# Seven steps of small products in a gated recurrence, gathered into three, with four more gathers on GpSimd

## The reference

```python
def chunked_gated_recurrence(q, k, log_f, v):
    """S_t = diag(f_t) S_{t-1} + k_t v_t^T,  o_t = S_t^T q_t  (chunkwise form)."""
    ...

def hgrn2_mixer(h, w_in, w_out, g_norm_w, lb_fwd, lb_bwd):
    """Bidirectional HGRN2. Single combined input projection partitioned into
    [q | f_fwd | f_bwd | i | g]; one scan per direction, summed; gated RMSNorm; output projection."""
    ...
    o = rmsnorm(o, g_norm_w) * jax.nn.silu(gh.astype(jnp.float32))
    return o.reshape(B_, L, D).astype(h.dtype) @ w_out
```

## Time and profile before

| | us |
|---|---|
| median of 3 runs | 2721.85 (2720.99 to 2722.36) |
| the profiled execution | 2721.11 |
| its span, first to last instruction | 2718.9 |
| TensorE busy | 2700.7 (99%) |
| DVE busy | 1966.1 (72%) |
| ACT busy | 1331.5 (49%) |
| GpSimd busy | 89.6 (3%) |
| DMA, mean over the span | 177 GB/s |

### The profile page before, as it was taken

One profiled execution on the slowest core, in us unless ns is written; L12 is line 12 of the kernel. 1 busy time (PEld: TensorE's weight loads), 2 busy tenths in 40 slices (PEclk: granted clock), 3 DMA queues, 4 the chain that ended last, 5 costly groups with the idle time before them and its releaser, 6 DMA issues.

```text
span 2718.9 us, 47515 instructions
## 1 busy us (share of the span) xinstructions
PE 2700.7 (99%) x17654; PEld 2300.9 (85%) x17654; DVE 1966.1 (72%) x2745; ACT 1331.5 (49%) x1674; POOL 89.6 (3%) x106
## 2 busy tenths in 40 slices
PE   9999999999999999999999999999999999999998
PEld 8888888878888888888888888878888888888887
DVE  6888888878888888644466687767678888885444
ACT  6444555455444444433465556666554444443343
POOL 0111111110000000000000000000000000000000
PEclk9999999999999999999999999999999999999999
DMA  7544444464555555655645544345455555555554
GB/s 244 177 163 163 164 160 158 160 199 165 189 185 185 185 191 190 191 186 188 220 146 171 170 142 139 132 156 185 151 178 191 193 192 190 186 185 190 185 186 152
DMA packets 136198, 481.69 MB, mean 177 GB/s; under 512 B 14880, under 2 KB 19120, under 8 KB 135680
## 3 DMA queue, kind: packets, MB, share of 16 engines
q1 hardware_dynamic: 134160, 472.06, 52.1%
q0 software_dynamic: 1376, 7.46, 0.8%
q10 hardware_dynamic: 528, 0.26, 0.0%
HBM read 477.63 MB, written 2.10 MB: 176 GB/s over the span
## 4 chain that ended last, share of the span: by engine, by line
PE 88%; DVE 5%; ACT 3%; issue 2%; DMA 2%; DVEq 0%; POOL 0%; ACTq 0%; SPq 0%
PE acc L418 34%; PE acc L420 17%; PE acc L441 8%; PE acc L442 8%; PE acc L443 8%; PE acc L389 4%; PE acc L391 2%; DVE wts L336 2%; DMA raw<-stream 1%; ACT wts L330 1%; PE ps L1378 1%; PE ps L716 1%; DVE cy L2240 1%; PE acc L903 1%; PE acc L536 0%
## 5 line engine op out<-in xcount | busy, mean ns | idle before, releaser
L418 PE MATMUL acc<-hs,wts 128*128 128x512 f32 x4640 | 1631.5, 395 | 0.1
L336 DVE TENSOR_TENSOR wts<-raw,wts 128x1024 fp32r<-128x1024 f32 x888 | 1058.3, 1222 | 536.9 <-ACT wts L330 535.6
L330 ACT ACTIVATE wts<-raw 128x1024 fp32r<-128x1024 f32 x888 | 913.2, 1054 | 877.0 <-PE acc L420 394.4
L420 PE MATMUL acc<-hs,wts 128*128 128x256 f32 x4640 | 1297.0, 280 | 0.0
L418 PEld LDWEIGHTS acc<-hs,wts 128*128 128x128 f32 x4640 | 870.8, 188 | 193.4 <-issue 0.7
L420 PEld LDWEIGHTS acc<-hs,wts 128*128 128x128 f32 x4640 | 871.5, 188 | 0.8 <-issue 0.7
L441 PE MATMUL acc<-wts,acts 128*128 128x512 f32 x688 | 273.2, 397 | 0.4 <-DVE wts L336 0.4
L442 PE MATMUL acc<-wts,acts 128*128 128x512 f32 x688 | 272.1, 395 | 0.0
L443 PE MATMUL acc<-wts,acts 128*128 128x512 f32 x688 | 270.5, 393 | 0.0
L344 ACT ACTIVATE half<-acc 128x512 f32<-128x512 f32 x161 | 95.4, 593 | 170.6 <-PE acc L420 151.3
L441 PEld LDWEIGHTS acc<-wts,acts 128*128 128x128 f32 x688 | 129.2, 188 | 32.7 <-DVE wts L336 1.3
(11 more groups left out here) (351 smaller groups left out, 2143.1 us busy)
## 6 DMA issues: line engine op xcount, KB each, us to landing
raw<-stream SPq DMA_DIRECT2D x888, 512.0 KB, 4.1
xf<-xT SPq DMA_DIRECT2D x8, 256.0 KB, 6.7
raw<-stream SPq DMA_DIRECT2D x8, 256.0 KB, 6.8
fw<-stream POOLq DMA_DIRECT2D x2, 1024.0 KB, 6.2
fm<-memT POOLq DMA_DIRECT2D x2, 1024.0 KB, 9.1
memr<-memT POOLq DMA_DIRECT2D x1, 2048.0 KB, 9.3
outT<-memr SPq DMA_DIRECT2D x7, 256.0 KB, 2.9
KQ<-masks POOLq DMA_DIRECT2D x1, 448.0 KB, 5.8
```

The costliest lines, as they stand in the source:

```text
L330: nc.scalar.activation(whi[:, b, :], raw[:, b, :], ACT.Copy).then_inc(hi_ready, 1)
L336: nc.vector.tensor_tensor(wlo[:, b, :], raw[:, b, :], whi[:, b, :].bitcast(F32), ALU.subtract).then_inc(lo_ready, 1)
L418: nc.tensor.matmul(acc[:, 2 * par + n, :], whi[:, b, c:c + P], src[:, kt, :], start=start, stop=False)
L420: mm = nc.tensor.matmul(acc[:, 2 * par + n, 0:T], wlo[:, b, c:c + P], src[:, kt, 0:T], start=False, stop=stop)
```

## The change

Levels 1 to 6 no longer have a step each on TensorE: levels 1, 2 and 3 are multiplied at place 21, levels 4, 5 and 6 at place 33. So that DVE can go on changing `KQ` meanwhile, GpSimd gathers also the queries of levels 1, 2, 4 and 5 into buffers of their own (`KM` has six instead of two; level 3's keys go to `sig[:, 2]`), and DVE's update of these levels waits for that gather instead of for TensorE; levels 3 and 6 still wait for TensorE, since their queries are read in place. The masked copies are spread anew: level 0's at its update, 1 at level 3's update, 2 one place later, 3 after level 4's, 4, 5 and 6 after level 6's. ACT copies the diagonal at place 4 instead of 5. The gain chain of DVE (`hg_vector_gain`) is apart from the low half of the squares and comes behind the recurrence's piece in its place 7, before at place 6 and ahead of it. `W` is packed more tightly to make room. Arithmetic and results are the same; so are all large products.

```diff
-        hg_pool = Steps(sem("hg_pool"), names("k0 q0 k1 k2 k3 k4 k5 k6"))
+        hg_pool = Steps(sem("hg_pool"), names("k0 q0 k1 q1 k2 q2 k3 k4 q4 k5 q5 k6"))
...
+        key_at, query_at = (0, 2, 4, 6, 0, 2, 4), (1, 3, 5, None, 1, 3, None)
+        level_bank = (3, 2, 3, 1, 2, 3, 1)
+
+        def gathered(i):
+
+            return KM[:, i] if i < 6 else sig[:, 2]
...
                 if lv:
                     dve.wait_ge(hg_vec.sem, hg_vec.count(f"w{lv}", turn))
-                dve.wait_ge(hg_pe.sem, hg_pe.count(f"g{lv}", turn))
+                if lv in (0, 3, 6):
+                    dve.wait_ge(hg_pe.sem, hg_pe.count(f"g{lv}", turn))
+                else:
+                    dve.wait_ge(hg_pool.sem, hg_pool.count(f"q{lv}", turn))
                 nc.vector.tensor_tensor(lower, lower, sibling(lv, 0), ALU.mult).then_inc(hg_vec.sem, 1)
                 nc.vector.tensor_tensor(upper, upper, sibling(lv, 1), ALU.mult).then_inc(hg_vec.sem, 1)
-                merge(dve, turn, lv)
+                if lv in (0, 3, 6):
+                    merge(dve, turn, (0, 1, 4)[lv // 3])
                 if not last or lv % 2:
                     yield
+                if lv in (3, 4, 6):
+                    merge(dve, turn, {3: 2, 4: 3, 6: 5}[lv])
                 if lv + 2 < LEVELS:
                     dve.wait_ge(hg_vec.sem, hg_vec.count(f"w{lv + 1}", turn))
                     whole_blocks(lv + 2).then_inc(hg_vec.sem, 1)
-                yield
...
+                if not last or lv < 6:
+                    yield
+            merge(dve, turn, 6)
...
         def hg_scalar(act, turn, par, last=False):
-            yield from pause(4)
+            yield from pause(3)
...
+        def hg_level(lv):
+
+            size = min(64, max(32, 1 << lv))
+            for s in range(0, 2 * T, size):
+                w = slice(s, s + size)
+                side = s // size % 2
+                n = w if lv < 5 else slice(s - size, s) if side else slice(s + size, s + 2 * size)
+                if query_at[lv] is not None:
+                    moving = gathered(query_at[lv])[:, n]
+                elif lv < 5:
+                    moving = queries(s, 1 << lv)
+                else:
+                    moving = KQ[:, 2 - side, n]
+                mm = nc.tensor.matmul(ps[s % P:s % P + size, level_bank[lv], n], gathered(key_at[lv])[:, w], moving,
+                                      start=True, stop=True)
+            mm.then_inc(hg_pe.sem, 1)
...
-            yield from pause(5 if last else 6)
-            for lv in range(1, LEVELS):
...
+            yield from pause(11 if last else 14)
+            pe.wait_ge(hg_pool.sem, hg_pool.count("k3", turn))
+            pe.wait_ge(hg_vec.sem, hg_vec.count("c0", turn))
+            if turn:
+                pe.wait_ge(hg_act_out.sem, hg_act_out.count("oln", turn - 1))
+            for lv in (1, 2, 3):
+                hg_level(lv)
+            yield from pause(9 if last else 12)
+            pe.wait_ge(hg_pool.sem, hg_pool.count("k6", turn))
+            pe.wait_ge(hg_vec.sem, hg_vec.count("c3", turn))
+            for lv in (4, 5, 6):
+                hg_level(lv)
+            yield from pause(3 if last else 4)
...
                     nc.gpsimd.tensor_copy(
-                        KM[:, lv % 2].rearrange("p (n u h) -> p n u h", u=2, h=1 << lv),
+                        gathered(key_at[lv]).rearrange("p (n u h) -> p n u h", u=2, h=1 << lv),
                         keys(1 << lv)).then_inc(hg_pool.sem, 1)
...
+                    if lv not in (3, 6):
+                        if lv == 0:
+                            pool.wait_ge(hg_vec.sem, hg_vec.count("qf", turn))
+                        nc.gpsimd.tensor_copy(
+                            gathered(query_at[lv]).rearrange("p (n u h) -> p n u h", u=2, h=1 << lv),
+                            all_queries(1 << lv)).then_inc(hg_pool.sem, 1)
```

More of the change, by code:

```diff
@@ L163, in build @@
             KQ = sb("KQ", [P, 4, 2 * T], F32, st)
-            W = sb("W", [P, LEVELS - 1, 2, T], F32, st)
-            KM = sb("KM", [P, 2, 2 * T], F32, st)
+            W = sb("W", [P, 4 * T], F32, st)
+            KM = sb("KM", [P, 6, 2 * T], F32, st)
             out_sq = sb("out_sq", [P, 2 * T], F32, st)[:]
@@ L1288, in hg_vector, with hg_vector_low @@
                     whole_blocks(lv + 2).then_inc(hg_vec.sem, 1)
-                yield
-        def hg_vector_out(dve, turn, par, late=False):
-            n = hin[:, par]
+                if not last or lv < 6:
+                    yield
+            merge(dve, turn, 6)
+        def hg_vector_low(dve, turn):
             yield from pause(2)
@@ L1296, in hg_vector_out, with hg_vector_gain @@
                                     ALU.subtract).then_inc(hg_vec_out.sem, 1)
-            yield from pause(4 if late else 3)
+        def hg_vector_gain(dve, turn, par, steps=6):
+            n = hin[:, par]
+            yield from pause(steps)
             dve.wait_ge(hg_act_out.sem, hg_act_out.count("or", turn))
@@ L1329, in hg_scalar @@
         def hg_scalar(act, turn, par, last=False):
-            yield from pause(4)
+            yield from pause(3)
             act.wait_ge(hg_pe.sem, hg_pe.count("diag", turn))
             nc.scalar.activation(AD[:].rearrange("p a b -> p (a b)"), ps[:, 1, :], ACT.Copy).then_inc(hg_act.sem, 1)
-            yield from pause(11 if last else 15)
+            yield from pause(12 if last else 16)
             act.wait_ge(hg_pe.sem, hg_pe.count("l128", turn))
@@ L1447, in hg_stage, with hg_all @@
             drain(side)
-        def hg_all(eng, what, take_in, attend, put_out):
+        def hg_all(eng, what, take_in, attend, put_out, finish=None):
             n = 2 if what == "pe" else 1
@@ L1456, in hg_all @@
             for t in range(2, 8):
-                hg_stage(eng, what, t, t % 2, slots(20 * n, put_out(eng, t - 2, t % 2),
-                                                    attend(eng, t - 1, 1 - t % 2),
-                                                    take_in(eng, t, t % 2)))
+                if what == "dve":
+                    side = slots(20, put_out(eng, t - 2), attend(eng, t - 1, 1 - t % 2),
+                                 finish(eng, t - 2, t % 2), take_in(eng, t, t % 2))
+                else:
+                    side = slots(20 * n, put_out(eng, t - 2, t % 2), attend(eng, t - 1, 1 - t % 2),
+                                 take_in(eng, t, t % 2))
+                hg_stage(eng, what, t, t % 2, side)
             def last_head():
                 yield from attend(eng, 7, 1, True)
-                yield from put_out(eng, 7, 1, *([True] if what == "pe" else []))
+                if what == "dve":
+                    yield from put_out(eng, 7)
+                    yield from finish(eng, 7, 1, 3)
+                else:
+                    yield from put_out(eng, 7, 1, *([True] if what == "pe" else []))
             def last_turn():
@@ L1468, in last_turn @@
                 elif what == "dve":
-                    yield from slots(24 * n, put_out(eng, 6, 0, True), last_head())
+                    yield from slots(24 * n, put_out(eng, 6), last_head(), finish(eng, 6, 0))
                 else:
```

17 lines of the change are left out of this document (7 added, 10 removed).

## The result

| | before | after |
|---|---|---|
| median (us) | 2722.53 (2720.99 to 2723.28, 8 runs) | 2729.29 (2725.43 to 2733.09, 8 runs) |
| the profiled execution | 2721.11 | 2728.14 |
| its span | 2718.9 | 2725.9 |
| mean granted clock of TensorE | 0.999 | 0.997 |

The ratio is 1.0026, with a 95% interval of 1.0016 to 1.0036. Forecast was no measurable change, 2723.5 in a range of 2712 to 2727.5; the time lies 1.8 us above that range. The runs after also spread more, 7.7 us against 2.3.

A forecast was written before the change was run, and what follows sets the result against it. TensorE, busy 2700.7 of 2718.9 us, was taken as the bound. Turn 0 -1.18, turns 1 to 6 +1.2 and turn 7 +1.95 gave +2.0: 2723.1 from the profiled execution, 2723.8 on the median, forecast 2723.5, range 2712 to 2727.5.

The forecast's parts named there:

- turn 0: First mixer turn, no gain chain beside it and no wait: joined steps save their full 1.18 us.
- turns 1 to 6, steps and waits: Each turn: 1.38 us more wait for level 3's gather, 1.18 less for joined steps; +0.20 each, +1.2 together.
- turn 7, steps and waits for the gather: Last turn: start of levels 1 to 3 1.95 us later, then +0.60, -1.19 and +0.60 for sets and steps: +1.95.
- The 0.48 us of ACT's copy: Diagonal's copy ahead of ACT's logarithm and exponential no longer delays two high halves: DVE's chain 0.48 us sooner.
- a third set: Third set of small products behind two others in one TensorE step: 0.30 us, like the second; 0.595 at the far end.
- the bound given was 0.30: Change from 32 to 64 columns inside the last step: at most 0.30 us a turn, left out of the sum.
- a wait of 2.49 in place of 1.11, 1.38 more: TensorE's wait for level 3's keys' gather at the step of levels 1 to 3; bounds 0.70 and 3.2 us.
- the three terms named for it, -0.61, +1.33 and +1.2: Turn 7, DVE's chain: a merge lost -0.61, two holds +1.33, last gather waiting for a low half +1.2 us.
- Nothing blocks: Rival: gathers stay 0.62 us and cost DVE nothing; -11.3 us, 2710.5; chance 0.17.
- Three steps cost three: Rival: three sets behind each other on TensorE cost three steps; +9.4 us, 2733; chance 0.02.
- Only the last gather waits: Rival: the queries' gather slips into a DVE gap, 0.6 less in 7 turns; -4.2 against the forecast, 2719.3; chance 0.20.
- The slower rival: Rival: gain chain's first piece is held too, +0.67 in each of turns 1 to 6 and turn 7; 2728.2; chance 0.11.

The follow-up runs named there:

- the first experiment: The changed kernel with DVE's low half of the squares put back behind the next pair of weight low halves in the last turn: 2725.74 us, ratio 1.0016.
- the masked-copy experiment: The changed kernel with level 0's masked copy moved from behind level 0's update to behind level 2's: 2716.43 us, ratio 0.9981.

## Why the prediction was wrong

**The sum, term by term**, in us on the two profiled executions:

| | put | measured |
|---|---|---|
| turn 0 | -1.18 | -1.07 |
| turns 1 to 6, steps and waits | +1.2 | -1.05 |
| turn 7, steps and waits for the gather | +1.95 | +1.38 |
| TensorE's clock behind the waits | nothing | +5.39 |
| the squares' low half | nothing | +1.83 |
| ahead of turn 0, and behind the output product | nothing | +0.5 |
| together | +2.0 | +7.0 |

**What held.** The mechanism on which the forecast rested is shown: gathers of GpSimd and pieces of DVE with two SBUF operands hold each other up, the change took away the merges that had stood beside the gathers, and the longer wait eats most of the joined steps' gain. Its sizes in turns 1 to 6: 2.00 us lost at the step where 2.49 was put, so that a turn without a fallen clock is 0.17 shorter, not 0.20 longer. Level 3's gather lasted 1.55 us, not the 1.79 of a row of level 0's, and the queries' gather held DVE for 0.39 and not 0.60. The 0.48 us of ACT's copy were exact. These misses lie on the other side from what failed: without the two missing terms the sum would have come out at -0.2, so part of the nearness to the range is luck.

**The steps.** TensorE across the first joined step in turn 0 (answers to the earlier trace rows), and across the second (answers to the earlier trace rows):

```profile
97.66 0.28 PE L420 MATMUL acc<-hs,wts 128*128 128x256 f32 x1
97.87 0.75 PE L1380 MATMUL ps<-KM 128*32 128x32 f32 x63
...
99.20 0.28 PE L420 MATMUL acc<-hs,wts 128*128 128x256 f32 x1
```

```profile
115.53 0.27 PE L391 MATMUL acc<-wts,hs 128*128 128x256 f32 x1
115.74 0.76 PE L1380 MATMUL ps<-KM 128*32 128x32 f32 x64
116.43 0.69 PE L1380 MATMUL ps<-KQ,KM 128*64 128x64 f32 x16
...
117.39 0.28 PE L391 MATMUL acc<-wts,hs 128*128 128x256 f32 x1
```

1.54 - 0.345 = 1.195 us for levels 1 to 3, as put: a third set costs 0.30 as the second does. Levels 4 to 6 cost 1.86 - 0.345 = 1.515 against 1.415. Those 0.10 us more are what a change from 32 to 64 columns inside the step could have cost; the bound given was 0.30. The saving is 1.08 a turn for 1.18.

**What failed, first: the clock.** The working of the wait and of the last turn priced a wait of 2.5 us and of nearly 4 us at their own length. The step "a wait of 2.49 in place of 1.11, 1.38 more" has a second term, what TensorE's clock does afterwards. In the profile before no wait exceeded 1.05 us in the mixer and no clock fell there, so its rows gave no price, and no bound was set for it. It measured 1.4 us in each of two turns and 2.6 in the last: 5.4 of the 7 us. The experiment with matmuls in the gap settles that it is the standing still. It falls after some of the waits only, and after other ones in another execution. That fits the wider spread: of the eight runs of the changed kernel the slowest, 2733.09 us, has the lowest mean clock, 0.995, and the fastest, 2725.43, has 0.997. Why one wait of 1.93 us brings it down and the next does not stays open.

**Second: the squares.** The text on the last turn counted merges, holds and steps, and not that DVE's generator ends without a last `yield`, so that L1311 moves ahead of two weight low halves. It was there to read in the order of DVE behind the last three masked copies. It costs a wait of 1.55 us in the profile, 1.83 us on the whole stretch, and the first experiment gives it back.

**The last turn itself** came out a little better than put: the step began 1.27 us later against the diagonal where 1.95 was put (the three terms named for it, -0.61, +1.33 and +1.2, come to 1.92).

**The rivals.** Nothing blocks: out, by the gathers of 1.55 and the masked-copy experiment. Three steps cost three: out. Only the last gather waits: out, since the gain chain's L1322 was held 0.39 us beside the queries' gather. The slower rival had the sign but the wrong mechanism; the gain's first piece, with one operand in PSUM, took 0.75 beside a gather, as elsewhere. The 0.12 given to slower was too little because every rival was a shift of one wait; none was a consequence of a wait.

What stays open: which of the waits near 2 us bring the clock down, and the 1.3 us behind the mixer.

## What to carry to other kernels

When a wait grows on an engine that was never idle for long, price what its clock does afterwards as well as the wait, and test it by filling the gap with work of no use. The same gather on GpSimd took 0.62 or 1.55 us here, by what stood beside it on DVE: read each of its copies together with DVE's piece in the row above, and when pieces are moved, ask which of them was the cover. And before steps are joined to save their overhead, move the late piece: two moves, one on ACT and one on DVE, gave 6 us here, and the joined steps gained only at a place where their inputs were ready.

## What the runs showed of the hardware

- After waits of TensorE of 1.93 us the granted clock went to half for 3.41 us in 2 of 6 turns (in two kernels, other turns each). Of two waits of 3.05 and 3.06 us, one had it at half for 6.83 us and the other not at all; with waits of 1.98 and 2.3 us it fell for 3.41. With the waits up to 1.55 us between 60 and 2700 us it fell in none of these profiles. The Trainium skill (TensorE: Matmul & The Clock Gate, Part 1: The HAM clock gate) states that the clock's share is set by how busy TensorE has been recently; these windows agree.
- Half clock for 3.41 us cost 1.4 us a turn (65.76 against 64.37), and for 6.83 us, 0.64 of it in the wait, 2.6 us (16.38 against 13.78).
- A gather on GpSimd and a two-operand piece on DVE exclude each other, and the one that comes second waits until the other is done: 1.55 for 0.62 us behind a low half. GpSimd's hold on DVE was 0.67 us for level 0's gather, whose runs are one element, and 0.35 to 0.42 for the others that DVE's next piece waited out in turn 3 and in the last turn (L1253 and L1322 in turn 3, a second low half in the last: 1.63 for 1.21). A DVE piece that reads one operand from PSUM ran beside a gather without loss (L1320, 0.75 us beside it and 0.74 elsewhere).
- The Trainium skill (SBUF — State Buffer, SBUF: two separate sides) states that exclusion, for a DVE instruction with two SBUF inputs and a GpSimd one that reads SBUF, and the runs agree, with the numbers above.
